# Low parts of 112 weight tiles: an accumulating DMA on GpSimd's queue in place of a subtraction on VectorE

## The chip, the cores and the metric

The kernel runs on one core of one Trainium2 chip. The metric is the device time of one execution in microseconds (us). Before the change it is 2673.17 us, the median of three executions (2671.55 to 2673.41).

## The reference

The reference is one inference step of a two-layer backbone, in float32. 640 token rows pass through it: 512 latent tokens (a grid of 8 by 64) and 128 context tokens. In each layer come:

1. a half-step SwiGLU feed-forward block: `(silu(g) * a) @ w_down` with `a, g = split(u @ w_up)`, model width 1024 and hidden width 2816;
2. token mixing from one input projection `[q | k | v | fourier | gate_A | gate_B]`: a 2-D Fourier transform branch, a neighbourhood attention branch (8 heads of 64), their gated sum, and an output projection `w_out`;
3. a second feed-forward block like the first.

Each sub-layer's input is `x * (1 + scale) + shift` and its output goes through `LN(ALPHA * x + gate * sub(x))`. The scales, shifts and gates are products of two condition vectors with `w_ada`. The outputs are the tokens and the context's keys and values.

## The kernel before, in words

**Split products.** TensorE multiplies in the format fp32r, which keeps fewer bits than float32. So each operand is held as a rounded high part and a low part (operand minus high part), and each product is made of three matmuls: high by high, high by low, low by high.

**Weight tiles.** All weights of one execution form a stream of 184 tiles, 92 per layer. A tile is 128 partitions by 16 blocks of 128 columns: 8 KB per partition, 1 MB in all. TensorE consumes them in a fixed order. A tile goes through these steps:

- SP's queue loads it from HBM into one of two buffers `w_raw[0]`, `w_raw[1]`. The load of tile t waits until the split of tile t-2 is done (semaphore `w_split`, `s_wsplit`).
- ScalarE writes the rounded copy `w_hi` (`round_tile`, L1039) and raises `w_hi_done` (`s_whi`). Before that it waits until TensorE has started the tile that frees the target buffer (`w_tile_started`, `s_wstart`).
- VectorE writes `w_lo = w_raw - w_hi` (`low_tile`, L1471) and raises `w_split`.
- TensorE waits for `w_split` before the tile's first matmul (`take`).

`w_hi` and `w_lo` have two buffers each. At the ends of the sub-layers further tiles go to spare buffers (`spare_f`, `spare_g`, `spare_h`, `spare_v`, `spare_o`), so that three or four tiles can be ready together.

**Two kinds of tiles.** 64 of the 184 tiles belong to the middle and last third of the up projections. They are multiplied by a scheme of seven half-size products instead of eight (`seven_products`), and are rounded and split in pieces of 512 columns with sums between them (`round_operand`, L1055; `low_operand`, L1485). The other 120 tiles are ordinary: rounded whole, split whole.

**Order of a layer.** A feed-forward block has three groups of hidden columns (6, 8 and 8 tiles up, and after each group the tiles down: 3, 4, 4). Group 0's up tiles are ordinary, those of groups 1 and 2 are `seven_products`. The last down projection is done half of the tokens after the other (`down_halves`, L557), so that each of its four tiles gets 48 matmuls first and 48 later; the layer norm of the first half runs beside the second. The next sub-layer then begins with two tiles used together (`both`, L598). The mixing block has five tiles and an attention run for each half of the heads (`attention`), then a loop of 12 tiles for gates and branches (`gates`, L975 and L991), and `w_out` by `down_halves` with four tiles.

**Engine programs.** Each engine's instructions stand in a fixed order written out by hand, and the engines meet only in semaphores. In VectorE's program `low_tile` stands between the evacuations of PSUM, the layer norm and the `w_ada` products (`ada_pair`, L1552 and L1554); in ScalarE's program `round_tile` stands between activations, Exp and the issue of `w_ada` loads. GpSimd has no work.

Of the kernel before, what the change touches and what calls it, by code (L numbers as in the profile page):

```python
# [99 lines left out]
def build(nc, a):  # L100
    ctx = ExitStack()
    with ctx:
# [190 lines left out]
        s_whi = sem("w_hi_done")  # L293
        s_wsplit = sem("w_split")
        s_wstart = sem("w_tile_started")
        s_aload = [sem(f"ada_loaded{s}") for s in range(2)]
# [71 lines left out]
        def make(which, **other):  # L368

            per = dict(PER_LAYER)  # L370
            sems = dict(
                tile=s_wstart, use=s_free, full=s_full, func=s_func, h=s_h, mods=s_mods, u32=s_u32,
                sum=s_sum, added=s_added, sqsum=s_sqsum, var=s_var, std=s_std, u=s_u, mean=s_mean, xc=s_xc, sq=s_sq, xn=s_xn, y=s_y, att=s_att, max=s_max,
                sc=s_sc, exp=s_exp, of=s_of, fill=s_fill, fev=s_fev, pt=s_pt, ptc=s_ptc, o=s_o, mix=s_mix, mrg=s_mrg,
                kv=s_kv, ada=s_adone, dve=s_dve, wraw=s_wload[0], whi=s_whi, wsum=s_wsum,
                ophi=s_ophi, opsplit=s_opsplit, prod=s_prod, snap=s_snap, late=s_late, add=s_add, hsum=s_hsum, hhi=s_hhi,
                tsum=s_tsum, thi=s_thi, tlow=s_tlow)
            first = dict(use=4, tile=1, ada=1, u=2 * KD, u32=2 * KD, mrg=4, add=1) | other
            return {k: Count(sems[k], per[k], first.get(k, 0)) for k in which}
# [3 lines left out]
        def _(sp):  # L383
# [54 lines left out]
            sp.wait_ge(s_out, 16 * 2 * KD)  # L438


# [578 lines left out]
        def _(act):  # L1019
# [3 lines left out]

            def round_tile(back=0, spare=None):


                r = raw_slot[0]
                raw_slot[0] ^= 1
                if r == 0:
                    C["wraw"].next(16)  # L1030
                act.wait_ge(s_wload[r], C["wraw"].at())
                C["whi"].next()
                act.wait_ge(s_wstart, C["whi"].at(back))
                if spare is None:
                    hi = w_hi[:, w_slot[0], :, :]
                    w_slot[0] ^= 1
                else:
                    hi = spare[0][:, :, :]
                act.activation(hi, w_raw[:, r, :, :], ACT.Copy).then_inc(s_whi, 1)  # L1039
# [214 lines left out]
            def opening():  # L1254

                def first_input(h, k):
                    i = 2 * k + h
                    if h == 0:
                        act.wait_ge(s_x[k], 16)
                    act.wait_ge(s_first, first_mods_ready(h, k))  # L1260
                    if h == 0 and k >= 4:
                        act.wait_ge(s_u, i - 7)
                    for lo, hi, v in SEGS[h]:
                        q = act.activation(u32_opening(h, k)[:, lo - h * HT:hi - h * HT], X[:, k, lo:hi],
                                           ACT.Identity, bias=mods[0][:, v, k:k + 1],
                                           scale=mods[0][:, v, KD + k:KD + k + 1])
# [16 lines left out]
                round_tile()  # L1283
                round_tile(1)
                for k in range(KD):
                    for h in range(2):
                        first_input(h, k)
                    if k == KD - 2:
                        round_tile(2, spare_f)
                for _ in range(3):  # L1290
                    gate_half()
                round_tile(2, spare_h)
# [156 lines left out]
        def _(dve):  # L1449
# [3 lines left out]

            w_slot, raw_slot = [0], [0]

            def low_tile(spare=None):
# [210 lines left out]
            def last_products(l, s, next_q, spares, more, places, late=()):  # L1667

                nxt = (s + 1) % 3
                dve.wait_ge(s_free, use.at())  # L1670
                low_tile()
                for pair in range(KD // 2):
                    add_pair(mods[s], 0, pair)
                    if pair < len(spares):
                        low_tile(spares[pair])
# [7 lines left out]
                if more:  # L1683
                    between[0] = [low_tile] + between[0] + [low_tile]
                normalise(0, between, not more)
# [23 lines left out]
            def down_of_six(m, next_pair, finish):  # L1709

                next_pair()
                finish()
                first = {1: low_tile, 2: lambda: token_sums(2), 3: low_tile, 4: lambda: token_sums(3),
                         5: first_operands, 7: next_pair}
# [7 lines left out]
            def down_loop(m, ada, counts):  # L1722
                for i in range(2):
                    down(m, lambda n: i * 4 + n, 4, [ada] * counts[i],
                         (low_tile, low_tile if i == 0 else first_operands))

# [31 lines left out]
            def seven_products(at, operands):  # L1758
# [14 lines left out]
                else:  # L1773
                    low_tile()
                dve.wait_ge(s_prod, C["prod"].at(-6))
# [21 lines left out]
            def first_up(chunks):  # L1797
                low_tile(spare_f)
                low_tile(spare_h)
                made = [product() for _ in range(2)]  # L1800
# [6 lines left out]
                evacuate(1, 1)  # L1807
                low_tile()
                chunks(0)(0)
# [4 lines left out]
            def opening(chunks):  # L1814
# [60 lines left out]
                evacuate(2, 0)  # L1875
                low_tile()
                chunks(0)(0)
# [17 lines left out]
            def ffn(l, s):  # L1895
# [17 lines left out]
                for group, size in enumerate(GROUPS):  # L1913
                    done = EARLY * (group == 0)

                    if group == 0:
                        dve.wait_ge(s_wstart, l * TILES + (TILES - 33) * (s == 2) + EARLY + 2)
                        low_tile()
                        evacuate(done, 0)
# [3 lines left out]
                        split_token_sums(0)  # L1923
                        low_tile()
                        evacuate(done + 1, 0)
# [18 lines left out]
            def attention(hh):  # L1944

                recip_at, bias_at = {}, {}
                for n in range(STEPS + 2):
# [40 lines left out]
                    if n in (2, 7):  # L1988
                        low_tile()
                C["pt"].next(4)  # L1990
# [45 lines left out]
            def mixing(l):  # L2036
                low_tile(spare_v)
                link(dve.memset(bm[:, :, 256:384], 0.0))
# [4 lines left out]
                for m, dst in enumerate((qT, kT)):  # L2043
                    rows(dst, 1, -ATTN_SCALE if m == 0 else 1.0)
                low_tile()
                for t in range(2, 5):
                    value(t)
                for hh in range(2):
                    if hh == 1:
                        low_tile()  # L2050
                        for m in range(4):
                            if m == 2:
                                low_tile()
                            u = use_no[0]
# [7 lines left out]
                        for t in range(5):  # L2062
                            if t == 1:
                                low_tile()
                            value(t)
# [13 lines left out]
                def gates(i):  # L2079
                    for pair in range(2):  # L2080
                        for e in range(4):
                            if e % 2 == 0:
                                low_tile()
                            dve.wait_ge(s_func, C["func"].next())
# [8 lines left out]
                        low_tile()  # L2093
                        for m in range(2):
# [41 lines left out]
    pt=UNITS, ptc=UNITS, o=UNITS, of=UNITS, fill=2 * PIECES, fev=2 * PIECES, mix=1, mrg=2 * KD, kv=64,  # L2136
    ada=3 * ADA_SUB, dve=359, wraw=8 * TILES, whi=TILES, wsum=8 * SEVEN, ophi=12 * SEVEN, opsplit=12 * SEVEN,
    prod=14 * SEVEN, snap=8 * SEVEN, late=2 * SEVEN, hsum=4 * SEVEN, hhi=4 * SEVEN, add=4 * SEVEN, tsum=48, thi=8, tlow=8)
# [126 lines left out]
```

## Time and profile before

| | |
|---|---|
| median of three executions | 2673.17 us |
| span of the profiled execution, first to last instruction | 2671.0 us |
| TensorE matmul busy | 2616.2 us (98%) |
| VectorE busy | 2068.0 us (77%) |
| ScalarE busy | 1059.4 us (40%) |
| GpSimd busy | 0.2 us |
| mean granted TensorE clock | 0.993 of full speed |
| DMA, mean over the span | 111 GB/s |

The profiled execution has no time of its own beside its span; the median lies 2.2 us above that span, which is what lies around it. "Busy" counts the time in which at least one instruction of the engine runs; matmuls are pipelined, so a single one lasts 0.31 us in the rows while one follows the other every 0.146 us.

### The profile page before, as it was taken

What the parts mean: (1) busy time and instruction counts of PE and PEld (TensorE: products, weight loads), DVE (VectorE), ACT (ScalarE), POOL (GpSimd) and SP (SyncE); (2) the same over time, 40 slices, a digit from 0 to 9 for tenths busy, and PEclk for the clock granted to TensorE, in tenths of its full rate; (3) what the DMA queues carried; (4) which work ended last, traced back from release to release, by engine and by line L of the source; (5) the groups of instructions that cost most, each with busy time, mean ns of one, the idle gap of its engine ahead of it and who ended that gap; (6) DMA issues with size and microseconds to landing.
All of it is one profiled execution on the core that took longest, in us unless ns stands there. A gap on an engine that the chain in (4) does not pass through costs nothing.

```text
span 2671.0 us, 46210 instructions
## 1 busy us (share of the span) xinstructions
PE 2616.2 (98%) x18004; PEld 2588.5 (97%) x18004; DVE 2068.0 (77%) x3924; ACT 1059.4 (40%) x1866; POOL 0.2 (0%) x4
## 2 busy tenths in 40 slices
PE   8999999899999999999999999999999999999997
PEld 8999999898999999999999999998999999999996
DVE  7787986767766888798689888786786568988876
ACT  5145253533222534525352534535242225253452
POOL 0000000000000000000000000000000000000000
PEclk9999999999999999999999999999999999999998
DMA  7433422223333132242223243221413322324321
GB/s 280 136 110 115 157 93 95 91 86 102 116 126 121 69 111 95 100 154 93 95 100 114 89 156 110 97 94 60 144 64 127 133 72 100 114 89 157 108 95 56
DMA packets 77804, 295.38 MB, mean 111 GB/s; under 512 B 25168, under 2 KB 31568, under 8 KB 54096
## 3 DMA queue, kind: packets, MB, share of 16 engines
q1 hardware_dynamic: 51552, 211.16, 22.5%
q10 hardware_dynamic: 26096, 82.16, 9.0%
q8 instruction: 96, 1.57, 0.2%
q14 instruction: 60, 0.49, 0.1%
HBM read 289.62 MB, written 6.82 MB: 111 GB/s over the span
## 4 chain that ended last, share of the span: by engine, by line
PE 94%; DVE 3%; DMA 1%; ACT 1%; issue 1%; ACTq 0%; SPq 0%; DVEq 0%
PE psum L709 10%; PE psum L714 10%; PE psum L713 10%; PE psum L512 5%; PE psum L514 5%; PE psum L515 5%; PE psum L560 4%; PE psum L561 4%; PE psum L557 4%; PE psum L975 3%; PE psum L977 3%; PE psum L978 3%; PE psum L598 2%; PE psum L602 2%; PE psum L603 2%; PE psum L810 2%
## 5 line engine op out<-in xcount | busy, mean ns | idle before, releaser
L714 PE MATMUL psum<-Th,w_lo 128*128 128x320 f32 x1024 | 316.4, 309 | 0.0
L709 PE MATMUL psum<-Th,w_hi 128*128 128x320 f32 x1024 | 316.3, 309 | 0.0
L713 PE MATMUL psum<-Tl,w_hi 128*128 128x320 f32 x1024 | 316.1, 309 | 0.0
L1039 ACT ACTIVATE w_hi<-w_raw 128x2048 fp32r<-128x2048 f32 x98 | 187.3, 1912 | 309.9 <-DVE acc L1554 155.9
L512 PE MATMUL psum<-Hh,w_hi 128*128 128x320 f32 x896 | 277.2, 309 | 3.3 <-DVE Hl L1742 2.4
L515 PE MATMUL psum<-Hh,w_lo 128*128 128x320 f32 x896 | 276.7, 309 | 0.0
L514 PE MATMUL psum<-Hl,w_hi 128*128 128x320 f32 x896 | 276.7, 309 | 0.0
L1471 DVE TENSOR_TENSOR w_lo<-w_raw,w_hi 128x2048 fp32r<-128x2048 f32 x98 | 224.3, 2289 | 55.1 <-ACT w_hi L1039 54.6
L709 PE MATMUL psum<-Uh,w_hi 128*128 128x320 f32 x768 | 237.5, 309 | 0.0
L713 PE MATMUL psum<-Ul,w_hi 128*128 128x320 f32 x768 | 237.2, 309 | 0.0
L714 PE MATMUL psum<-Uh,w_lo 128*128 128x320 f32 x768 | 236.6, 308 | 0.0
L1552 DVE CUSTOM_DVE_ANT_0 junk<-ada_w,csilu 128x1024 bf16<-128x1024 f32 x144 | 176.1, 1223 | 70.7 <-DVEq L2087 48.5
L1055 ACT ACTIVATE w_hi<-sums 128x512 fp32r<-128x512 f32 x256 | 160.1, 628 | 145.5 <-PE psum L709 57.0
L1485 DVE TENSOR_TENSOR w_lo<-sums,w_hi 128x512 fp32r<-128x512 f32 x256 | 170.2, 688 | 42.8 <-ACT w_hi L1055 41.5
L714 PEld LDWEIGHTS psum<-Th,w_lo 128*128 128x128 f32 x1024 | 192.6, 188 | 0.0
L713 PEld LDWEIGHTS psum<-Tl,w_hi 128*128 128x128 f32 x1024 | 192.5, 188 | 0.0
L709 PEld LDWEIGHTS psum<-Th,w_hi 128*128 128x128 f32 x1024 | 192.5, 188 | 0.0
L1554 DVE CUSTOM_DVE_ANT_0 junk<-ada_w,csilu 128x1024 bf16<-128x1024 f32 x144 | 176.4, 1225 | 5.0
L1070 ACT ACTIVATE snaps<-psum 128x320 f32<-128x320 f32 x256 | 111.9, 437 | 156.4 <-PE psum L714 151.9
L512 PEld LDWEIGHTS psum<-Hh,w_hi 128*128 128x128 f32 x896 | 168.4, 188 | 4.2 <-DVE Hl L1742 2.6
L514 PEld LDWEIGHTS psum<-Hl,w_hi 128*128 128x128 f32 x896 | 168.5, 188 | 0.0
L515 PEld LDWEIGHTS psum<-Hh,w_lo 128*128 128x128 f32 x896 | 168.4, 188 | 0.0
(283 smaller groups left out, 7248.2 us busy)
## 6 DMA issues: line engine op xcount, KB each, us to landing
w_raw<-in_wstream SPq DMA_DIRECT2D x184, 1024.0 KB, 4.8
ada_w<-in_ada ACTq DMA_DIRECT2D x145, 512.0 KB, 3.4
first_w<-in_ada SPq DMA_DIRECT2D x9, 512.0 KB, 14.5
first_w<-in_ada_first SPq DMA_DIRECT2D x6, 512.0 KB, 9.3
gath<-in_rpb SPq DMA_DIRECT2D x128, 24.0 KB, 3.5
G<-gath ACTq DMA_DIRECT2D x4, 768.0 KB, 4.5
X<-in_xT SPq DMA_DIRECT2D x8, 320.0 KB, 15.2
yT<-X SPq DMA_DIRECT2D x16, 160.0 KB, 1.8
```

The costliest lines, as they stand in the source:

```text
L512: m1 = pe.matmul(out, wh, rh, start=(k == 0), stop=False)
L514: pe.matmul(out, wh, rl, start=False, stop=False)
L515: mm = pe.matmul(out, wl, rh, start=False, stop=(k == nk - 1))
L709: m1 = pe.matmul(out, hi[:, k, :], rh, start=(start and k == 0), stop=False, skip_group_check=not start)
L713: pe.matmul(out, hi[:, k, :], rl, start=False, stop=False, skip_group_check=not start)
L714: mm = pe.matmul(out, lo[:, k, :], rh, start=False, stop=(k == 3), skip_group_check=not start)
L1039: act.activation(hi, w_raw[:, r, :, :], ACT.Copy).then_inc(s_whi, 1)
L1055: act.activation(two_rows(operand(w_hi, j, w_slot[0])), operand_source(op_raw[0], j), ACT.Copy)\
L1471: dve.tensor_tensor(lo, w_raw[:, r, :, :], hi.bitcast(F32), ALU.subtract).then_inc(s_wsplit, 1)
L1485: dve.tensor_tensor(two_rows(operand(w_lo, j, w_slot[0])), operand_source(op_raw[0], j), two_rows(operand(w_hi, j, w_slot[0])).bitcast(F32 ...
L1552: link(dve.tensor_tensor_reduce(junk[:, :], ada_w[:, s, :], csilu[:, 0, :], 1.0, 0.0, ALU.mult, ALU.add, acc4[:, 0, s:s + 1]))
L1554: i = dve.tensor_tensor_reduce(junk[:, :], ada_w[:, s, :], csilu[:, 1, :], 1.0, 0.0, ALU.mult, ALU.add, acc4[:, 1, s:s + 1])
```

## The change

For 112 of the 120 ordinary tiles VectorE no longer writes the low part. ScalarE first writes the negated rounded tile into the low part's buffer and then the rounded tile as before. GpSimd's new program waits for `w_hi_done`, issues a DMA from `w_raw` to the low buffer that adds (`accum_op=ADD`; 1 MB, both in SBUF), waits until it has landed, and raises `w_split`. It issues one DMA at a time, in the order of the stream. The eight tiles that stay with VectorE are the first four of the kernel and the four whose low part lies in `u_rows`. On VectorE `low_tile` becomes `low_on_pool`, which only counts, except for those. The DMA descriptor scratch grows from 64 to 512 bytes per partition.

```diff
+        @block.gpsimd
+        def _(pool):
+            C = make(["whi", "wlow"])
+            def add_low(spare=None):
+                r = raw_slot[0]
+                raw_slot[0] ^= 1
+                if spare is None:
+                    lo = w_lo[:, w_slot[0], :, :]
+                    w_slot[0] ^= 1
+                else:
+                    lo = spare[1][:, :, :]
+                pool.wait_ge(s_whi, C["whi"].next())
+                pool.dma_start(lo.bitcast(F32), w_raw[:, r, :, :], accum_op=ALU.add).then_inc(s_wlow, 16)
+                pool.wait_ge(s_wlow, C["wlow"].next(16))
+                pool.wait_ge(s_wsplit, C["whi"].at(1))
+                pool.sem_inc(s_wsplit, 1)
...
@@ ScalarE
-            def round_tile(back=0, spare=None):
+            def round_tile(back=0, spare=None, on_vector=False):
...
+                if not on_vector:
+                    act.activation(lo, w_raw[:, r, :, :], ACT.Copy, scale=-1.0)
                 act.activation(hi, w_raw[:, r, :, :], ACT.Copy).then_inc(s_whi, 1)
...
@@ VectorE
+            def low_on_pool(spare=None):
+                if spare is not None and spare[1] is None:
+                    dve.wait_ge(s_wsplit, C["whi"].at())
+                    low_tile(spare)
+                    return
+                raw_slot[0] ^= 1
+                w_slot[0] ^= spare is None
+                C["whi"].next()
...
-                low_tile()
+                low_on_pool()
...
-    nc = _bacc.Bacc("TRN2", target_bir_lowering=False, num_devices=1, dynamic_dma_scratch_size=64)
+    nc = _bacc.Bacc("TRN2", target_bir_lowering=False, num_devices=1, dynamic_dma_scratch_size=512)
```

## Rows read from the trace of the kernel before

**Rows 1.** The page, parts 1 and 2: busy us by engine; granted clock in 40 slices.
```profile
PE 2616.2 (98%) x18004; PEld 2588.5 (97%) x18004; DVE 2068.0 (77%) x3924; ACT 1059.4 (40%) x1866; POOL 0.2 (0%) x4
PEclk9999999999999999999999999999999999999998
```

**Rows 2.** The page, part 4: the chain that ended last, by engine.
```profile
PE 94%; DVE 3%; DMA 1%; ACT 1%; issue 1%; ACTq 0%; SPq 0%; DVEq 0%
```

**Rows 3.** Waits of PE, longest total: engine, line, releaser: total us, times, longest.
```profile
PE psum L598 <- DVE Ul L1590: 10.8, 2, 5.4
```

**Rows 4.** Tile w_raw, first and last of five L1471 groups: ns min/median/max, first and last start.
```profile
L1039 ACT ACTIVATE w_hi<-w_raw x98: 1896/1915/1922, 17.1 to 2593.2; 128x2048 fp32r<-128x2048 f32 x98
L1471 DVE TENSOR_TENSOR w_lo<-w_raw,w_hi x98: 2277/2291/2305, 19.0 to 2595.3; 128x2048 fp32r<-128x2048 f32 x98
...
L1471 DVE TENSOR_TENSOR spare_o_lo<-w_raw,spare_o_hi x4: 2291/2291/2292, 854.8 to 2169.3; 128x2048 fp32r<-128x2048 f32 x4
```

**Rows 5.** The page, part 6: DMA issues, count, KB each, median us to landing.
```profile
w_raw<-in_wstream SPq DMA_DIRECT2D x184, 1024.0 KB, 4.8
...
yT<-X SPq DMA_DIRECT2D x16, 160.0 KB, 1.8
```

**Rows 6.** Timeline, end of the third group's seven-product run: start us, us, engine, line.
```profile
411.52 1.92 ACT L1039 ACTIVATE w_hi<-w_raw 128x2048 fp32r<-128x2048 f32 x1 [1.32 <-PE psum L714]
...
414.20 2.28 DVE L1471 TENSOR_TENSOR w_lo<-w_raw,w_hi 128x2048 fp32r<-128x2048 f32 x1
...
416.64 0.38 PE L557 MATMUL psum<-Hh,w_hi 128*128 128x320 f32 x1
...
430.79 0.30 PE L557 MATMUL psum<-Hh,spare_f_hi 128*128 128x320 f32 x1
```

**Rows 7.** Timeline, two tiles before a sub-layer's first matmuls.
```profile
460.64 1.91 ACT L1039 ACTIVATE w_hi<-w_raw 128x2048 fp32r<-128x2048 f32 x1
...
464.86 1.90 ACT L1039 ACTIVATE w_hi<-w_raw 128x2048 fp32r<-128x2048 f32 x1
...
474.09 0.31 PE L598 MATMUL psum<-Uh,w_hi 128*128 128x320 f32 x1
```

**Rows 8.** Timeline, the tiles of w_out.
```profile
846.37 1.92 ACT L1039 ACTIVATE w_hi<-w_raw 128x2048 fp32r<-128x2048 f32 x1 [11.64 <-PE psum L557]
...
853.00 0.31 PE L557 MATMUL psum<-Mh,w_hi 128*128 128x320 f32 x1
...
867.07 0.31 PE L557 MATMUL psum<-Mh,spare_o_hi 128*128 128x320 f32 x1
```

**Rows 9.** Timeline, single tiles: a first down projection, and the same of the opening.
```profile
981.02 1.90 ACT L1039 ACTIVATE w_hi<-w_raw 128x2048 fp32r<-128x2048 f32 x1
...
989.10 0.31 PE L512 MATMUL psum<-Hh,w_hi 128*128 128x320 f32 x1
...
113.19 1.90 ACT L1039 ACTIVATE w_hi<-w_raw 128x2048 fp32r<-128x2048 f32 x1
...
117.56 0.38 PE L512 MATMUL psum<-Hh,w_hi 128*128 128x320 f32 x1 [0.42 <-DVE w_lo L1471]
```

**Rows 10.** Timeline, a tile of the gates loop.
```profile
706.10 1.92 ACT L1039 ACTIVATE w_hi<-w_raw 128x2048 fp32r<-128x2048 f32 x1
...
719.25 0.31 PE L975 MATMUL psum<-Uh,w_hi 128*128 128x320 f32 x1
```

**Rows 11.** The chain in order of time, inside an attention run: start us, us, what.
```profile
661.97 2.27 DVE w_lo L1471
```

**Rows 12.** Timeline and stretches after PE's longest idle: us, busy (count) by engine, then clock.
```profile
501.98 0.60 PE L598 MATMUL psum<-Uh,w_hi 128*128 128x320 f32 x1 [5.42 <-DVE Ul L1590]
...
502.00:504.00 2.00, 2.00 (x8) 2.00 (x9) 1.46 (x5) 1.93 (x6) 0.00 (x0) 0.50 0.00 0
504.00:506.00 2.00, 2.00 (x10) 2.00 (x10) 1.67 (x5) 1.97 (x4) 0.00 (x0) 0.56 0.00 0
506.00:508.00 2.00, 2.00 (x15) 2.00 (x15) 1.65 (x5) 1.94 (x6) 0.00 (x0) 1.00 0.00 0
```

More of the change, by code:

```diff
@@ L438, in _, with split_elsewhere, last_products, ffn @@
             sp.wait_ge(s_out, 16 * 2 * KD)
+        @block.gpsimd
+        def _(pool):
+            C = make(["whi", "wlow"])
+            raw_slot, w_slot = [0], [0]
+            def add_low(spare=None):
[11 more added lines that the diff above has]
+                pool.sem_inc(s_wsplit, 1)
+            def split_elsewhere(n):
+                raw_slot[0] ^= n % 2
+                C["whi"].next(n)
+            def last_products(spares, more):
+                add_low()
+                for spare in spares:
+                    if spare[1] is None:
+                        split_elsewhere(1)
+                    else:
+                        add_low(spare)
+                if more:
+                    add_low()
+                    add_low()
+            def ffn(first, last):
+                if first:
+                    split_elsewhere(4)
+                else:
+                    add_low(spare_f)
+                    add_low(spare_h)
+                for _ in range(5):
+                    add_low()
+                split_elsewhere(8)
+                for _ in range(4):
+                    add_low()
+                split_elsewhere(8)
+                add_low()
+                last_products([spare_f, spare_g], not last)
+            def mixing():
+                add_low(spare_v)
+                for _ in range(1 + 2 + 3 + 2 + 12):
+                    add_low()
+                last_products(spare_o, True)
+            for l in range(DEPTH):
+                ffn(l == 0, False)
+                mixing()
+                ffn(False, l == DEPTH - 1)
+            check_counts(C.values())
         @block.tensor
@@ L1034, in round_tile @@
                 if spare is None:
-                    hi = w_hi[:, w_slot[0], :, :]
+                    hi, lo = w_hi[:, w_slot[0], :, :], w_lo[:, w_slot[0], :, :]
                     w_slot[0] ^= 1
-                else:
-                    hi = spare[0][:, :, :]
+                elif spare[1] is not None:
+                    hi, lo = [w[:, :, :] for w in spare]
+                else:
+                    hi, on_vector = spare[0][:, :, :], True
+                if not on_vector:
+                    act.activation(lo, w_raw[:, r, :, :], ACT.Copy, scale=-1.0)
                 act.activation(hi, w_raw[:, r, :, :], ACT.Copy).then_inc(s_whi, 1)
@@ L1674, in last_products @@
                     if pair < len(spares):
-                        low_tile(spares[pair])
+                        low_on_pool(spares[pair])
                     if 2 - len(late) <= pair < 2:
@@ L1683, in last_products @@
                 if more:
-                    between[0] = [low_tile] + between[0] + [low_tile]
+                    between[0] = [low_on_pool] + between[0] + [low_on_pool]
                 normalise(0, between, not more)
@@ L1712, in down_of_six @@
                 finish()
-                first = {1: low_tile, 2: lambda: token_sums(2), 3: low_tile, 4: lambda: token_sums(3),
+                first = {1: low_on_pool, 2: lambda: token_sums(2), 3: low_on_pool, 4: lambda: token_sums(3),
                          5: first_operands, 7: next_pair}
@@ L1773, in seven_products @@
                 else:
-                    low_tile()
+                    low_on_pool()
                 dve.wait_ge(s_prod, C["prod"].at(-6))
@@ L1797, in first_up @@
             def first_up(chunks):
-                low_tile(spare_f)
-                low_tile(spare_h)
+                low_on_pool(spare_f)
+                low_on_pool(spare_h)
                 made = [product() for _ in range(2)]
@@ L1807, in first_up @@
                 evacuate(1, 1)
-                low_tile()
+                low_on_pool()
                 chunks(0)(0)
@@ L1875, in opening @@
                 evacuate(2, 0)
-                low_tile()
+                low_on_pool()
                 chunks(0)(0)
@@ L1917, in ffn @@
                         dve.wait_ge(s_wstart, l * TILES + (TILES - 33) * (s == 2) + EARLY + 2)
-                        low_tile()
+                        low_on_pool()
                         evacuate(done, 0)
@@ L1923, in ffn @@
                         split_token_sums(0)
-                        low_tile()
+                        low_on_pool()
                         evacuate(done + 1, 0)
@@ L1988, in attention @@
                     if n in (2, 7):
-                        low_tile()
+                        low_on_pool()
                 C["pt"].next(4)
@@ L2036, in mixing @@
             def mixing(l):
-                low_tile(spare_v)
+                low_on_pool(spare_v)
                 link(dve.memset(bm[:, :, 256:384], 0.0))
@@ L2044, in mixing @@
                     rows(dst, 1, -ATTN_SCALE if m == 0 else 1.0)
-                low_tile()
+                low_on_pool()
                 for t in range(2, 5):
@@ L2063, in mixing @@
                             if t == 1:
-                                low_tile()
+                                low_on_pool()
                             value(t)
@@ L2082, in gates @@
                             if e % 2 == 0:
-                                low_tile()
+                                low_on_pool()
                             dve.wait_ge(s_func, C["func"].next())
@@ L2092, in gates @@
                                 ada_pair(mods[2], i * 8 + c, loads(l, base + c, i * 4))
-                        low_tile()
+                        low_on_pool()
                         for m in range(2):
```

19 lines of the change are left out of this document (10 added, 9 removed).

## The prediction, written before the change was run

> **What bounds the kernel now.** I read the page's busy times first. TensorE is busy for 2616.2 of 2671.0 us and its granted clock is at full speed in nearly every slice [rows 1]. The chain of waits says the same: 94% of it is PE [rows 2]. VectorE, at 2068.0 us busy, is no bound. The largest total of PE's waits is 10.8 us, and that one ends in the layer norm's output, not in a weight tile [rows 3]. So work taken off VectorE can return only what little of it stands on the chain, while everything that makes a weight tile ready later than TensorE reaches it is paid in full. The question for the change is therefore how much later a tile becomes ready, and how far ahead of TensorE each one is now.
>
> **What is removed and added.** VectorE loses 112 subtractions of 2.29 us, 256 us in all. The trace has 116 of them in five groups, of which the first four tiles of the kernel stay; the other four that stay are at another line [rows 4]. ScalarE gains 112 copies of 1.92 us, 215 us on an engine 40% busy. GpSimd gains 112 DMAs of 1 MB within SBUF that read the source, read the target and write the target. A tile was ready 1.92 + 2.29 = 4.2 us after ScalarE began it, if VectorE was free. Now it is ready 1.92 + 1.92 + L = 3.84 + L us after, with L the time from the DMA's issue to its landing, semaphores included.
>
> **L.** The trace has no accumulating DMA, none from GpSimd, and none within SBUF. The nearest rows are the load of a tile, 1024 KB landing in 4.8 us, and a store of 160 KB in 1.8 us [rows 5]. Their difference, 3.0 us for 864 KB, is 3.55 us per 1024 KB, and leaves 1.25 us that don't depend on the size. If the accumulation reads 2 MB on one path and writes 1 MB beside it, L is 1.25 + 2 * 3.55 = 8.35 us; I take 8.5 us. Below, 4.8 us is the plain copy. Above, three passes one after the other and a slower issue give 1.25 + 3 * 3.55 = 11.9, so 12 us. I take 8.5 because adding needs both operands read, and nothing shows that the write is serial to the reads.
>
> The loads of the next tiles and of w_ada run on the same DMA engines; I leave that inside this range.
>
> The Trainium skill bears on L at three places, none of which the trace of before can show. "Collectives: The Full Stack", section "The bandwidth ceiling: the fold count and why AG ≠ RS ≠ AR", says that the adding itself costs no time, and that a reduce runs at half the rate of a copy because it fetches from two sources. That is the form of my sum. "DMA: Bandwidth & Descriptors", "Anatomy of one DMA", gives 2.0 us plus bytes over 436 GB/s for a DMA from GpSimd; as an estimate with the bytes doubled that is 6.8 us, and the places below then give a time near 2770 us instead. "SBUF — State Buffer", "SBUF: two separate sides", says that VectorE's copies within SBUF can hold up GpSimd's descriptors, which speaks against the change and would lengthen L.
>
> **Where a tile becomes late.** For each kind of place I take ScalarE's start of the tile and the first matmul that needs it. How late it is follows as 3.84 + L minus that distance.
>
> - After each of the eight seven-product runs: 416.64 - 411.52 = 5.12 us, where ScalarE, VectorE (414.20 to 416.48) and TensorE now just meet [rows 6]. Late by L - 1.3 = 7.2 us. Eight times: 58 us.
> - Behind four of these come two more tiles for GpSimd, needed 7.05 us apart (third at 430.79 [rows 6]). The DMAs go one at a time, so the third lands at 3.84 + 3L, needed after 19.27: late by 3L - 15.4 = 10.1 us, of which 7.2 is counted. Four times 2.9: 12 us.
> - w_out, twice: first tile L - 2.8 = 5.7 us, third 3.84 + 3L - 20.70 = 8.6 us late [rows 8]. 17 us.
> - Two tiles together at the beginning of five sub-layers. Both are needed after 474.09 - 460.64 = 13.45 us, and the second DMA starts when the first has landed: late by 3.84 + 2L - 13.45 = 7.4 us [rows 7]. The second rounding, now at 464.86, would be through by 470.6 even if pushed back by the first negation, and isn't last. 37 us.
> - Single tiles that ScalarE begins late because of other work: in the first down projection of the three later feed-forward blocks, and by my reading four more in the mixing blocks with 0 to 0.5 us more or less room. 8.08 us of distance, late by 4.3 us [rows 9]. Seven times: 30 us. In the opening the same tile has 4.37 us: late by 8.0 us [rows 9].
> - The gates loop, 22 tiles: 719.25 - 706.10 = 13.15 us of distance [rows 10]. Late only if L is over 9.3 us; at 8.5 nothing. The tile period covers it.
> - The raw buffers are held longer, by the same 3.84 + L. A load of 4.8 us follows, and outside the bursts 14.1 us pass per tile, so the load stays hidden; in a burst the DMA that is waited for ends later than that load and the two copies.
>
> Sum: 58 + 12 + 17 + 37 + 30 + 8 = 162 us.
>
> **What comes back.** In the attention runs `low_tile` stands on the chain, 2.27 us in the row shown [rows 11]. ScalarE's extra 1.92 us stand before the Exp of the same runs. The net of eight such tiles lies between -18 us and +15 us; since VectorE and not ScalarE is last in the row shown, I take -9 us.
>
> **The clock.** After PE's idle of 5.42 us the granted clock is 0.50, its lower level of 1.2 GHz: 8 and 10 matmuls in two stretches of 2 us instead of 15 in each. 12 matmuls of 0.133 us are lost, 1.6 us [rows 12]. The new stalls over 5 us are 8 + 5 + 2 + 1 = 16: 26 us.
>
> Together 162 - 9 + 26 = 179 us on a span of 2671.0 us: 2850 us. The median shown lies 2.2 us above the span, so the time is 2852 us.
>
> **Rivals.**
>
> - *The DMA is as quick as a plain copy, L = 4.8 to 6 us.* For it: nothing here says that reading a second operand costs. Against it: it has to be read. At 4.8: 8 * 3.5 + 2 * 2.0 + 7 * 0.6 + 4.3 - 9 = 32 us, no stall over 5 us: 2705 us. At 6, by the same sum, 2740 us.
> - *The DMA is slow, L over 12 us,* from the adder or from descriptors written by software. At 12: 4 * 10.7 + 4 * 20.6 + 2 * 19.1 + 5 * 14.4 + 7 * 7.8 + 11.5, 22 tiles of the gates loop by 2.7 each, -9, and 24 slow restarts of 1.6 us come to 390 us: 3065 us. At 16 the loop tiles cost 6.7 each and it is about 3320 us. Only an unseen cost of GpSimd's path speaks for it.
> - *Faster than before.* The tiles' DMA would have to land within the time that VectorE took. The mechanism is VectorE's 256 us given back to the attention chain and to `ada_pair`, for which ScalarE waits before it rounds. It decides below L = 2.2 us, where 8 * 0.9 us of lateness and 1.7 us in the opening equal the 9 us returned. At L under 1.3 us the time is 2664 us. Against it: the shortest landing of 1 MB is 4.8 us and even 160 KB take 1.8 us [rows 5].
> - *The low parts aren't waited for as the diff says*, or the engines reorder so that lateness is absorbed: within 0.2% of before, 2673 us. The fixed order of the programs speaks against it.
>
> **How the numbers follow.** My forecast (L from 6 to 11 us) 0.60; quick copy 0.19; slow DMA 0.15; faster 0.04; no change 0.02. The range takes the quick copy at 4.8 us as its low end, 2700 us, and the 12 us case as its high end, 3060 us; beyond them stand most of the slow case and the two last ones. A difference under 0.2% (5 us) can't be told from none: faster 0.04, same 0.02, slower 0.94.
>
> **What would show it.** In the changed kernel's DMA part the new queue's median landing is L; 7.5 to 9.5 us confirms it. PE's waits should name the landing (or GpSimd) at L557 and L512 after the seven-product runs, eight times about 7 us, and at the sub-layers' first matmuls, five times about 7 us. The gates loop should show no waits. VectorE should be near 2068 - 256 = 1812 us busy and ScalarE near 1274 us; the mean granted clock should fall by about one in a hundred. The prediction fails if L is outside 6 to 11 us, if the DMAs overlap, or if the longer hold of the raw buffers delays the seven-product tiles too.

## The result, and the profile after

The changed kernel takes 2912.5 us (median; 2910.6 to 2914.2) against 2673.1 us for the kernel before on the same chip: a ratio of 1.0897, 95% interval 1.0882 to 1.0912. The span of the profiled execution is 2908.8 us, 237.8 us longer than before. The forecast was 2852 us: slower, as predicted, but by 239 us instead of 179.

The page of the changed kernel, parts 1 to 3 and 6 (answering to [rows 1, 5]):

```profile
span 2908.8 us, 46405 instructions
PE 2682.5 (92%) x18004; PEld 2642.8 (91%) x18004; DVE 1825.0 (63%) x3812; ACT 1260.7 (43%) x1978; POOL 100.4 (3%) x116
...
PEclk9999998899999999999999999999999999999998
...
q0 software_dynamic: 16128, 117.45, 20.7%
...
w_raw<-in_wstream SPq DMA_DIRECT2D x184, 1024.0 KB, 4.8
w_lo<-w_raw POOLq DMA_DIRECT2D x96, 1024.0 KB, 8.0
ada_w<-in_ada ACTq DMA_DIRECT2D x145, 512.0 KB, 5.3
spare_f_lo<-w_raw POOLq DMA_DIRECT2D x7, 1024.0 KB, 10.6
```

VectorE is 243 us less busy (1825 us; I had forecast 1812) and ScalarE 201 us more (1261 us; forecast 1274), and neither sets the time: TensorE's idle time (span less busy) went from 54.8 to 226.3 us, +171.5. Its busy time also grew, by 66.3 us, at an unchanged number of matmuls; with it went a lower granted clock (mean 0.964 instead of 0.993, where I had forecast a fall of one in a hundred).

PE's waits for GpSimd (line waited at, releaser: us in total, times, longest), where [rows 3] had nothing of the kind:

```profile
PE psum L621 <- POOLq L460: 64.7, 18, 5.1
PE psum L662 <- POOLq L460: 49.3, 5, 11.1
PE psum L576 <- POOLq L460: 25.8, 9, 6.6
PE psum L801 <- POOLq L460: 15.2, 5, 3.8
```

The end of the third group's seven-product run and the burst behind it, timeline (start us, us, engine, line; answering to [rows 6]):

```profile
424.29 1.92 ACT L1106 ACTIVATE w_lo<-w_raw 128x2048 fp32r<-128x2048 f32 x1 [1.32 <-PE psum L778]
426.11 1.89 ACT L1107 ACTIVATE w_hi<-w_raw 128x2048 fp32r<-128x2048 f32 x1
428.44 0.88 POOL L457 DMA_DIRECT2D w_lo<-w_raw  x1 [119.15 <-ACT w_hi L1107]
...
435.62 0.60 PE L621 MATMUL psum<-Hh,w_hi 128*128 128x320 f32 x1 [5.13 <-POOLq L460]
...
436.32 1.91 ACT L1106 ACTIVATE w_lo<-w_raw 128x2048 fp32r<-128x2048 f32 x1 [4.33 <-PE psum L621]
...
440.39 0.87 POOL L457 DMA_DIRECT2D w_lo<-w_raw  x1 [11.07 <-ACT w_hi L1107]
...
447.56 0.61 PE L621 MATMUL psum<-Hh,w_hi 128*128 128x320 f32 x1 [2.65 <-POOLq L460]
448.00 0.88 POOL L457 DMA_DIRECT2D spare_f_lo<-w_raw  x1 [6.74 <-POOLq L460]
...
459.17 0.38 PE L621 MATMUL psum<-Hh,spare_f_hi 128*128 128x320 f32 x1 [1.55 <-POOLq L460]
```

Two things are to be seen. From the first DMA's issue to the product it takes 7.2 us. And ScalarE begins the second tile only at 436.32, released by TensorE's first product of the first one, so the second DMA starts 12 us after the first, not as soon as the first has landed. The third tile's DMA, from 448.00, takes 11.0 us, with a raw load in flight.

In the table, the start of the first product of each of the 184 tiles is compared between the trace of before and that of the kernel named; what a tile adds to the distance is its cost, in us (early_add and plain_copy are experiments, below). With what comes behind the last tile this sums to 237.8 us for the changed kernel, the whole difference of the spans.

| place | forecast | changed | early_add | plain_copy |
|---|---|---|---|---|
| ends of the 8 seven-product runs | 58 | 43.9 | 28.7 | 23.3 |
| last tile of those runs | 0 | 6.8 | 6.8 | 6.8 |
| tiles behind the 4 runs without a burst | 0 | 13.8 | 14.5 | 7.3 |
| second and third tile of the 4 bursts | 12 | 37.3 | 33.2 | 17.6 |
| w_out, twice three tiles | 17 | 27.2 | 25.1 | 14.2 |
| 5 pairs, at their first product | 37 | 50.1 | 40.2 | 25.5 |
| products behind the pairs | 0 | 9.1 | 12.3 | 10.6 |
| single tiles | 30 | 43.3 | 28.6 | 17.9 |
| opening | 8 | 2.9 | -0.2 | -0.8 |
| attention | -9 | -3.0 | -7.5 | -7.4 |
| gates loop | 0 | 0.0 | 0.0 | 0.0 |
| rest (fourth tiles of the bursts and of w_out, the end) | 0 | 6.4 | 13.5 | 4.0 |
| clock, forecast apart, measured inside the rows above | 26 | | | |
| sum | 179 | 237.8 | 195.2 | 119.0 |

The profiled execution of early_add is the longest of its four, 9 us over their median, so its column is some 9 us too high.

### The profile page after: what moved, and what is told of

It is laid out like the page before. It is cut to its first block and busy times, and to the rows that moved or that the text cites. A ratio compares the mean times of both kernels' runs of the same rounds, so it can differ in the third digit from the quotient of the medians.

```text
span 2908.8 us, 46405 instructions
## 1 busy us (share of the span) xinstructions
PE 2682.5 (92%) x18004; PEld 2642.8 (91%) x18004; DVE 1825.0 (63%) x3812; ACT 1260.7 (43%) x1978; POOL 100.4 (3%) x116
## 5 line engine op out<-in xcount | busy, mean ns | idle before, releaser
L1106 ACT ACTIVATE w_lo<-w_raw 128x2048 fp32r<-128x2048 f32 x96 | 183.6, 1912 | 325.6 <-PE psum L576 106.1
L457 POOL DMA_DIRECT2D w_lo<-w_raw x96 | 86.2, 898 | 2573.8 <-ACT w_hi L1107 2536.4
## 6 DMA issues: line engine op xcount, KB each, us to landing
spare_f_lo<-w_raw POOLq DMA_DIRECT2D x7, 1024.0 KB, 10.6
first_w<-in_ada SPq DMA_DIRECT2D x9, 512.0 KB, 14.5
spare_o_lo<-w_raw POOLq DMA_DIRECT2D x4, 1024.0 KB, 10.7
```

What stands on the lines that cost most here:

```text
L1106: act.activation(lo, w_raw[:, r, :, :], ACT.Copy, scale=-1.0)
```

## The experiments

My theory after the result: the price is lateness of the low part at the places where the tile has under 13 us of room, and it follows the DMA's landing. The rivals: ScalarE's extra 215 us, or VectorE's work being on the path after all; and for the 60 us above the forecast, a clock that falls more often, or DMAs that are slower beside others.

**no_add.** GpSimd passes the semaphore on without any DMA, so the low part stays the negated tile.

```diff
-pool.dma_start(lo.bitcast(F32), w_raw[:, r, :, :], accum_op=ALU.add).then_inc(s_wlow, 16)
+pool.sem_inc(s_wlow, 16)
```

> GpSimd passes the semaphore on at once; the adding DMA is left out, so that the low parts hold only the negated rounded tile. Theory (a tile is late by its DMA, L = 7.4 us from ScalarE's end, and TensorE's clock falls after each stall): with L near 0.2 us all stalls go and VectorE's 256 us come back only in attention: 2655 to 2670 us. Rival (ScalarE's second copy, 1.92 us before every tile, does a good part of the harm): 2700 us or more.

Measured: 2672.96 us, ratio to before 1.0005 (0.9995 to 1.0014). That is 3 us above the theory's range and far below the rival's. By places, 6.8 us are lost at the last tiles of the seven-product runs and 2.2 at other places; 5.9 us come back in attention, 3.1 in the opening. They cancel. So all of the 239 us hang on the DMA, and the rival "faster than before" is ruled out even with a landing time of nothing. Of the 9 us that I forecast to come back in attention 5.9 are there, and what comes back is lost again to ScalarE's copy.

**plain_copy** and **half_add.** The same DMA without adding (the low part becomes the raw tile), and the addition of only 8 of the 16 blocks.

```diff
-pool.dma_start(lo.bitcast(F32), w_raw[:, r, :, :], accum_op=ALU.add).then_inc(s_wlow, 16)
+pool.dma_start(lo.bitcast(F32), w_raw[:, r, :, :]).then_inc(s_wlow, 16)                                   # plain_copy
+pool.dma_start(lo.bitcast(F32)[:, 0:8, :], w_raw[:, r, 0:8, :], accum_op=ALU.add).then_inc(s_wlow, 16)    # half_add
```

> The same DMA of 1 MB within SBUF from GpSimd, copying instead of adding; the sum is left out. Theory (adding halves the rate because two operands are read): packets of 8 KB take near 0.35 us instead of 0.64, landing falls from 7.0 to about 4.5 us, and the time to 2705 to 2725 us. Rival (GpSimd's path is slow whatever it does): landing stays at 7 us or more and the time above 2850 us.

> Adds only blocks 0 to 7 of each tile (512 KB), the other half of the sum is left out. Theory: landing = 1.8 us fixed + 5.1 us for 1 MB, so 4.4 us; time like plain_copy, 2705 to 2725 us. Rival (the fixed part, descriptors and semaphores, is most of L): landing above 5.5 us and time above 2770 us.

Measured: 2790.2 us (1.0440; 1.0423 to 1.0458) and 2783.5 us (1.0418; 1.0399 to 1.0437). The pages, plain_copy first (queue: packets, MB, share of 16 engines; then landing):

```profile
span 2790.0 us, 46405 instructions
...
q0 software_dynamic: 16128, 117.45, 10.9%
...
w_lo<-w_raw POOLq DMA_DIRECT2D x96, 1024.0 KB, 4.6
...
spare_f_lo<-w_raw POOLq DMA_DIRECT2D x7, 1024.0 KB, 8.6
```

```profile
span 2781.6 us, 46405 instructions
...
q0 software_dynamic: 16128, 58.73, 11.4%
...
w_lo<-w_raw POOLq DMA_DIRECT2D x96, 512.0 KB, 4.6
spare_f_lo<-w_raw POOLq DMA_DIRECT2D x7, 512.0 KB, 6.7
```

The engines' own time for one of the 112 DMAs is the share times the span: 0.207 * 2908.8 / 112 = 5.4 us with the addition, 0.109 * 2790.0 / 112 = 2.7 us as a copy, 0.114 * 2781.6 / 112 = 2.8 us for half. So adding costs as much as a second pass over the data, whatever the reason. The Trainium skill, "Collectives: The Full Stack", section "The bandwidth ceiling: the fold count and why AG ≠ RS ≠ AR", says of collectives between ranks that a reduction moves at half the rate of a copy; these rows agree for a DMA within SBUF, 5.4 to 2.7.

The landings came as expected, but both times lie above the theory's range, by 65 and 59 us; half_add's even lies in its rival's, though that rival's landing (above 5.5 us) did not come. The run ends came close (23.3 us for 28 by the forecast's formula at 4.8). But the pairs cost 25.5 us where 2L - 9.6 gives nothing: at the first pair the two copies land after 6.2 and 8.6 us, not twice 4.6, and all five second copies take 8.2 to 9.2 us, behind a raw load (see Pairs, below). And the burst's second tile costs 2.1 us each although a quick copy should catch up.

**early_add.** ScalarE signals after the negated copy, and GpSimd starts the DMA while the high part is still being written; it raises `w_split` when both are there.

```diff
-act.activation(lo, w_raw[:, r, :, :], ACT.Copy, scale=-1.0)
+act.activation(lo, w_raw[:, r, :, :], ACT.Copy, scale=-1.0).then_inc(s_wneg, 1)
...
-pool.wait_ge(s_whi, C["whi"].next())
+pool.wait_ge(s_wneg, C["wneg"].next())
+C["whi"].next()
...
 pool.wait_ge(s_wlow, C["wlow"].next(16))
+pool.wait_ge(s_whi, C["whi"].at())
```

> GpSimd starts the DMA after the negated copy, beside ScalarE's copy of the high part, and waits for both. The whole sum is computed. Theory (each late tile is late by 1.92 + 1.92 + L behind its gate): 1.92 us less at about 30 places where TensorE waits, and a little of the clock: 2835 to 2860 us. Rival (the DMAs are bound by each other and by the loads, so that an earlier start gains nothing): 2895 us or more.

Measured: 2859.0 us (1.0699; 1.0682 to 1.0717), as expected: 1.9 us per tile, taken off the path of the landing, are worth 53.5 us. The lateness is what costs. The rival, that an earlier start gains nothing, is ruled out.

**negate_only.** No DMA: ScalarE writes the negated copy as well, and VectorE subtracts as before.

```diff
             def low_on_pool(spare=None):
-                (counts the tile and leaves it to GpSimd)
+                low_tile(spare)
```

> No DMA at all: ScalarE still writes the negated copy before the rounded one, and VectorE subtracts as in the kernel before, 2.29 us each, 112 times. Leaving the DMA out and the subtraction too gave 2672.96 us, 0.05% over before. Theory: what the extra 1.92 us on ScalarE costs is what they cost where the tile's path had no room, as at the ends of seven-product runs: 8 * 1.9 us + one or two places of 1 to 2 us = 15 to 25 us, so 2688 to 2700 us. Rival: ScalarE's copy is hidden everywhere, since in the kernel without the DMA it was too: 2671 to 2677 us.

Measured: 2711.0 us (1.0144; 1.0129 to 1.0160), 11 us above the top of what I expected. 6.8 us are the last tiles of the seven-product runs, 0.85 us each, as in no_add and in every kernel with the copy: ScalarE takes its copy before the `snaps` that TensorE waits for. The run ends and bursts cost 10.5 us, two tiles of the mixing blocks 6.2, the first down projections of the later feed-forward blocks 10.9. PE's waits name ScalarE's copy (`snaps`, not among the listed waits of before) and VectorE, at `w_lo` and at its later work `Hl` (2.4 us in all before):

```profile
PE psum L710 <- ACT snaps L1075: 7.8, 11, 0.9
PE psum L513 <- DVE Hl L1750: 7.1, 4, 2.1
PE psum L513 <- DVE w_lo L1479: 6.1, 8, 2.2
PE psum L558 <- DVE w_lo L1479: 5.1, 8, 0.7
```

So the 1.92 us on ScalarE are dear when VectorE's 2.29 us follow them. In no_add they cost nothing on balance, with VectorE's work gone.

**two_at_once.** At the five pairs GpSimd issues both DMAs before it waits for the first.

```diff
+for (r, w), done in zip(slots, (s_wlow, s_wlow2)):
+    pool.wait_ge(s_whi, C["whi"].next())
+    pool.dma_start(w_lo[:, w, :, :].bitcast(F32), w_raw[:, r, :, :], accum_op=ALU.add).then_inc(done, 16)
```

> The changed kernel, but at the five pairs of tiles before a sub-layer GpSimd issues both DMAs before it waits for the first. Theory: the second tile is late by two whole latencies one after the other (8.8 + 10.8 us). Of each, about 5 us are the engines' own packets and 2 to 5 us are issue, completion and sharing; overlapped, the second lands 3 to 5 us sooner, five times, and two or three slow restarts become shorter: 2885 to 2898 us, against 2912.5 us. Rival 1: the sixteen DMA engines are what is full (the raw load and two accumulations together), so the second lands no sooner: 2908 to 2915 us. Rival 2: the first lands so much later beside the second that the pair is worse: over 2915 us.

Measured: 2918.2 us (1.0923; 1.0906 to 1.0940), no gain and perhaps 6 us worse (the intervals of the two ratios overlap). That is the second rival's range, though the first DMA landed no later than before, after 8.7 us. The five waits for the pairs total 50.7 us instead of 49.3, the longest 11.4 instead of 11.1:

```profile
PE psum L674 <- POOLq L473: 50.7, 5, 11.4
```

But the experiment did not bring about what it was to test. ScalarE had rounded the second tile by 497.52, and GpSimd's record of the second DMA begins only at 502.07, 0.3 us after the first landed; so it is at all five pairs (0.26 to 0.34 us):

```profile
493.12 0.87 POOL L467 DMA_DIRECT2D w_lo<-w_raw  x1 [46.06 <-ACT w_hi L1119]
...
495.62 1.90 ACT L1119 ACTIVATE w_hi<-w_raw 128x2048 fp32r<-128x2048 f32 x1
...
502.07 0.88 POOL L467 DMA_DIRECT2D w_lo<-w_raw  x1 [8.09 <-DMA w_lo<-w_raw]
```

The program's only wait between the two issues, for that rounding, was over by then; what held the second issue back is open. Whether two overlapping additions would gain anything is not tested.

**filled.** Matmuls of constants ahead of the wait for the first three tiles after a seven-product run, and likewise in w_out.

```diff
 if t == len(kept):
+    if t < 3:
+        for _ in range(28):
+            pe.matmul(bank(u, 0, 0, HT), cst_h[:, 0, :], half(mh, ml, h)(0)[0], start=True, stop=True)
     kept.append(take(spares[t - 2] if t >= 2 else None))
```

> It is early_add (2859.0 us) with 28 matmuls of constants, about 3.7 us at full speed, ahead of the wait for each of the first three tiles after a seven-product run and of the two w_out groups; they write a bank that the real products then start afresh. Theory: about 30 us of what the change costs aren't waiting but TensorE's clock, which falls after each stall of 3.5 us and more. With the stalls filled the clock stays at 2.4 GHz there: 18 places, of which some 12 now restart slowly by 1.6 us or more, give 20 to 35 us back: 2825 to 2840 us, mean granted clock 0.98 instead of 0.969. Rival: the longer busy time of TensorE has another source than the stalls (the DMAs' traffic in SBUF, say); then the clock stays near 0.969 and the fill only delays the products, 2859 to 2890 us.

That text has an error of mine: the kernel that ran is the changed kernel with this edit, without early_add's, and stands against 2912.5 us. Measured: 2926.7 us (1.0949; 1.0933 to 1.0966), 14 us more, where the theory had 20 to 35 us less. At the first stall of the burst the clock stayed up. The changed kernel and filled, stretches there (us, busy and count of PE, PEld, DVE, ACT, POOL, then PE's clock, DMA share, GB/s):

```profile
434.00:436.00 2.00, 0.38 (x1) 0.41 (x2) 0.00 (x0) 0.00 (x0) 0.00 (x0) 0.50 0.33 66
436.00:438.00 2.00, 2.00 (x9) 2.00 (x9) 0.00 (x0) 1.68 (x1) 0.00 (x0) 0.50 0.42 147
```

```profile
434.00:436.00 2.00, 1.30 (x9) 1.30 (x10) 0.00 (x0) 0.79 (x1) 0.00 (x0) 1.00 0.21 37
436.00:438.00 2.00, 2.00 (x15) 2.00 (x15) 0.00 (x0) 2.00 (x2) 0.00 (x0) 1.00 0.85 299
```

15 matmuls in 2 us instead of 9, at 2.4 GHz instead of 1.2. At the second stall, 2.47 us idle before 448.58, the clock fell to 0.50 all the same, and the mean clock rose only from 0.964 to 0.970. ScalarE began the second tile only 0.3 us sooner after the first, and its DMA took 9.2 us instead of 7.0. I take it that in a burst a faster TensorE mostly waits longer for the next tile, and that a fill which outlasts the wait delays the product; the runs do not separate the two.

**fill_pairs** and **fill_longer.** The same ahead of the five pairs, where no tile follows closely.

```diff
+us = [next_use(), next_use()]
+for _ in range(FILL):          # 56 in fill_pairs, 74 in fill_longer
+    pe.matmul(bank(us[0], 0, 0, 2 * P), cst_h[:, 0, :], cst_h[:, 0:2, :], start=True, stop=True)
 tiles = [take(), take()]
```

> The changed kernel (2912.5 us) with 56 matmuls of constants (256 columns, about 6 us at full speed) ahead of the wait for the pair of tiles, at the five sub-layer beginnings where TensorE waits 8.9 to 11.4 us; they write a bank that the real products start afresh. Theory: the products behind a pair take 2.2, 1.5, 1.7, 1.8 and 1.8 us longer than before the change, 9.1 us together, and that is the clock at 0.50 after the wait. With the wait filled the granted clock is 1.00 there and 7 to 10 us come back: 2902 to 2906 us. Rival: those products are slower for another reason (the raw load and the additions beside them), and the clock gives back only where nothing waits: 2910 to 2915 us with the clock at 1.00 in these stretches.

> fill_pairs (2910.2 us) with 74 matmuls of constants ahead of each pair of tiles instead of 56, some 2.2 us more. In fill_pairs 4.4, 3.2, 2.4 and 2.0 us of idle time were left behind the fill; in the first three of these the granted clock still fell to 0.50 and the products behind the pair took 1.6 to 2.5 us longer, in the last it stayed at 1.00 and they took as long as before the change. Theory: with 2.2 us less of idle time the clock stays at 1.00 at four or five pairs, and the 7.5 us of the products behind the pairs shrink to under 3 us: 2903 to 2908 us. Rival: the fill is too long at some pairs and delays them, or the clock falls all the same: 2909 to 2916 us.

Measured: 2910.2 us (1.0889; 1.0875 to 1.0904) and 2909.2 us (1.0884; 1.0869 to 1.0898), both above the theory's range and just inside the rival's. In fill_pairs 4.45 us of idle time were left at the first pair and the clock fell all the same. In fill_longer it is 1.32 us, and the clock stays. Its timeline and stretches there:

```profile
501.64 9.03 PE L656 MATMUL psum<-cst_h 128*128 128x256 f32 x74
511.99 0.38 PE L670 MATMUL psum<-Uh,w_hi 128*128 128x320 f32 x1 [1.32 <-POOLq L461]
```

```profile
512.00:514.00 2.00, 2.00 (x14) 2.00 (x15) 0.00 (x0) 1.53 (x1) 0.00 (x0) 1.00 0.54 94
514.00:516.00 2.00, 2.00 (x15) 2.00 (x15) 0.00 (x0) 2.00 (x2) 0.00 (x0) 1.00 0.92 381
```

The products behind the five pairs, 9.1 us longer than before in the changed kernel and 7.5 in fill_pairs, are 0.4 us longer in fill_longer. So that lengthening was the clock. Of the 8.7 us regained, the span kept 4.1 (2908.8 to 2904.7), and the medians differ by 3.3 us. What took the rest back lies in the bursts above all (3.3 us more than in the changed kernel, with longer landings); its cause is open. The intervals of the ratios overlap, so a gain in time is not established; the 8.7 us at the place itself are.

**mixed** and **att_only.** The DMA only where the room is some 13 us or more: the 8 tiles of the attention runs and the 24 of the gates loop (mixed), or the 8 alone (att_only). All others are split by VectorE, without the negated copy.

```diff
-round_tile()                    # everywhere but in attention (and gates, mixed)
+round_tile(on_vector=True)
...
-low_on_pool()                   # the same tiles, on VectorE
+low_tile()
```

> The accumulating DMA only where the tile is ready long before it is needed: the four tiles inside the attention runs and the twelve tiles of the gates loop of each layer, 32 tiles in all (13 us from ScalarE's start to the first product). The other 80 are split by VectorE as before, without the negated copy. Theory: a tile whose room is above 3.84 us plus the landing costs nothing, so PE waits for GpSimd nowhere over 0.5 us, and the time is that of before within 0.2%: 2668 to 2677 us; VectorE loses 73 us of work that isn't on the path. Rival 1: the attention stretches are bound by VectorE, 2.27 us per tile stood on the chain there, and 8 of them come back: 2655 to 2666 us. Rival 2: the DMAs cost by something else than lateness (traffic beside the loads, ScalarE's copies before the Exp): over 2682 us.

> Like mixed (2666.9 us), but the twelve tiles of the gates loop of each layer go back to VectorE: the accumulating DMA for the eight tiles of the attention runs alone. Theory: what mixed gains over before, 5.2 us, is VectorE's 2.27 us per tile taken off the chain in the attention runs, and the gates loop is bound by TensorE; so the gain stays whole, 2665 to 2669 us. Rival: part of it came from VectorE's 55 us less in the gates loop; then 2669 to 2672 us.

Measured: 2666.9 us (0.9981; 0.9972 to 0.9990) and 2666.3 us (0.9976; 0.9967 to 0.9985). Both beat the kernel before, by 5 to 7 us. mixed fell between its theory and its first rival, att_only where its theory had it, so the gates loop gives nothing back and costs nothing. The gain is a quarter of a per cent, with intervals that end just below 1. All of it is won at four of the eight tiles: in att_only 1.4, 1.1, 1.1 and 2.5 us, 6.0 us in sum. The chain of att_only in the run of [rows 11] (start us, us, what) goes on without the 2.27 us of `w_lo` at 661.97:

```profile
659.53 1.02 DVE bm L2039 x2
660.55 0.20 DVE Otok L2049
660.89 1.52 PE psum L860 x12
```

## Why the prediction was right, and where it was not

**What bounds.** Right. TensorE's waits took nearly the whole price; VectorE's 256 us gave back next to nothing.

**L.** I had 8.5 us with 7.1 us of them for two reads and 1.25 fixed. Alone, a DMA takes 7.0 us from its record to the semaphore (6.9 is the shortest landing, below), of which 5.1 us are eight packets of 8 KB on each engine, 0.64 us each (0.33 in plain_copy), 1.4 us go before the first and 0.3 after the last. At 40 of the 112 it lands within 7.1 us. The median is 8.0 us, and 9.7 to 12.2 where a raw load goes first, at 16 tiles: the second of each pair, the third of each burst, the last two of each w_out and the three of `spare_h`. The single value of 8.5 us came out near by luck, between two values that I had set inside one range and not worked out: it put the run ends too high and everything behind a load too low, and the two errors partly cancel in the total.

The Trainium skill, "DMA: Bandwidth & Descriptors", section "Anatomy of one DMA", gave 6.8 us as an estimate: near the 7.0 us of a DMA alone. Its time of 2770 us was too low for the reasons that plain_copy missed: the loads that go first, and waits that start again.

**Run ends.** Forecast 7.2 us each, measured 5.2 to 5.4 (one 6.8), 43.9 for 58: L was 7.0 here, and TensorE reached the tile 0.85 us later, which stands in the next row of the table.

**Bursts.** This is a step that failed: "The DMAs go one at a time, so the third lands at 3.84 + 3L", 2.9 us beyond the first's 7.2. ScalarE's rounding of the second tile waits for TensorE's start of the first (436.32, released by PE in the timeline), so after the stall 3.84 + L start again; and the third DMA takes 11.0 us. Measured 9.3 us per burst instead of 2.9. The same two things make w_out 27.2 instead of 17.

**Pairs.** The form 3.84 + 2L - 13.45 held but for 1.3 us between the steps: with 8.8 and 10.7 us for the two landings at the first pair it gives 9.9, and the pair was 11.3 us late instead of 7.4. The changed kernel's issues there:

```profile
493.24 0.87 POOL L457 DMA_DIRECT2D w_lo<-w_raw  x1 [44.37 <-ACT w_hi L1107]
502.69 0.89 POOL L457 DMA_DIRECT2D w_lo<-w_raw  x1 [8.58 <-POOLq L460]
```

```profile
513.80 0.61 PE L662 MATMUL psum<-Uh,w_hi 128*128 128x320 f32 x1 [11.10 <-POOLq L460]
```

Both the next raw load and GpSimd's next DMA are released by the `w_split` that follows the first landing, the load from 502.27 on. The load goes first, and the addition doesn't share with it but waits. The DMA queues in the stretches 502.7 to 507.2 and 507.2 to 513.5 (q1 is SP's loads, q0 GpSimd's; packets, MB, share of 16 engines):

```profile
q1 hardware_dynamic: 121, 0.99, 81.8%
```

```profile
q0 software_dynamic: 144, 1.05, 80.2%
q1 hardware_dynamic: 23, 0.06, 2.5%
```

So at all 16 tiles named under L: the first packet comes 3.5 to 4.6 us after the DMA's record instead of 1.4, and the packets themselves are no slower than alone (0.63 us). "I leave that inside this range" is the sentence that cost 13 us here.

**Single tiles.** 43.3 for 30. Four of them, in the mixing blocks, were taken at 4.3 us; the two before the second attention run cost 5.6 and 7.0. In the three later feed-forward blocks the tile I had priced, the first of the down projection, never waited for GpSimd: the tile before it did (L801, 3.3 to 3.7 us), and with that delay ScalarE began the priced tile 14.1 us before its first product (1055.19 and 1069.29) instead of 8.1. I had not listed the tile before. The opening cost 2.9 instead of 8: the tile before was itself 4.0 us late, so the one I had priced cost only 2.2 more, and the next gave 2.9 back.

**Gates loop and raw buffers.** Right: no tile of the loop moved, at landings of 7.0 to 8.2 us, under the limit of 9.3.

**What comes back.** I forecast -9 us in attention; no_add shows -5.9 there and the changed kernel -3.0. That the opening gives 3.1 more in no_add, which makes 9, is chance.

**The copy on ScalarE.** Not in the forecast beyond its 1.92 us per tile's path: 6.8 us at the last tiles of the runs.

**The clock.** 16 stalls over 5 us at 1.6 us each, 26 us, was a mis-sized term: TensorE's busy time grew by 66.3 us. In the timeline above a stall of 2.65 us at 447.56 is followed by matmuls at 0.50 as well, and the four lines of PE's waits above count 37 waits for GpSimd, not 16. But busy time isn't time: at the pairs 8.7 us less of it brought 4.1, in the bursts none that could be seen. The 66.3 and the 171.5 add up to 237.8, and still the clock's own price in time may be less than 66; only at the pairs was it measured. How the 59 us above the forecast divide between the clock and later landings is open for the rest.

**Rivals.** The quick copy was ruled out by the landing (8.0), and the slow DMA too; no change by the measured time, and faster by no_add. The rule of the page "SBUF — State Buffer" of the Trainium skill, section "SBUF: two separate sides", that VectorE's copies hold up GpSimd's descriptors, was seen once. Of 112 issues nearly all take 0.86 to 0.9 us, and one, in the opening, 2.6: it began inside VectorE's one operation on the whole of `X` and ended just after it. In plain_copy, half_add, two_at_once and fill_pairs it is the same; in early_add the issue came before that operation and took 0.89 us. The tile is the one of the opening that was 4.0 us late; its DMA's first packet came 3.2 us after the record instead of 1.4. It is no large price, since the whole opening cost 2.9 us. (The two in the timeline; then GpSimd's issues: ns min/median/max, and the landings of all.)

```profile
97.11 2.82 DVE L1969 TENSOR_SCALAR X<-X 128x5120 f32<-128x5120 f32 x1
97.46 2.62 POOL L457 DMA_DIRECT2D w_lo<-w_raw  x1 [30.37 <-ACT w_hi L1107]
```

```profile
L457 POOL DMA_DIRECT2D w_lo<-w_raw x96: 859/872/2615, 66.1 to 2823.5; - x96
...
DMA to landing us min/median/max: 6.9/8.0/12.2
```

## What to carry over

Work taken from an engine that isn't last is worth what of it stands on the chain, here 6 of 256 us, and a slower path for the same data is paid at every place with less room than its latency. List the room of each tile and move only those that have more: four of the eight in attention carried all the gain, the 24 of the gates loop changed nothing, and the other 80 carried the loss. Price a DMA by what goes ahead of it at that place, and after every new stall look at which waits start again from the delayed engine. And look in the trace whether an experiment did what its edit says before reading its time.

## What the hardware showed that I had not expected

- An accumulating DMA within SBUF takes 5.4 us of each engine's time per 1 MB, a copy 2.7, half an addition 2.8. Alone the semaphore comes 7.0, 4.5 and 4.6 us after the issue. In bursts, w_out and pairs, where a raw tile's load is released at the same moment, the load's packets go first: 9.7 to 12.2 us with adding and 7.1 to 10.0 us without.
- Issuing both additions of a pair without a wait between them did not overlap them: the second's record began 0.26 to 0.34 us after the first had landed, five times of five.
- One issue on GpSimd took 2.6 us instead of 0.87, inside a VectorE operation of 2.8 us within SBUF.
- The loads pay too: `ada_w`, 512 KB, lands after 5.3 us in the changed kernel, 4.3 in plain_copy, 3.4 before.
- TensorE's clock fell to 0.50 after waits of 2.7 and 4.4 us, and stayed at 1.00 after one of 1.3 us; but in the changed kernel it also stayed at 1.00 after waits of 2.8 and 2.9 us (1404.21 and 667.06). Matmuls of constants in the wait kept it up, but were worth at most 4 us of span where five pairs were filled.
